# Splits of weights, a tree of squares and one bank: a reordered start of three stages in a hybrid decoder layer

## The chip, the cores and the metric

One core of one Trainium2 chip. The metric is the device time of one execution in microseconds (us); lower is better. TensorE, VectorE (DVE), ScalarE (ACT) and GpSimd (POOL) work side by side, each through its own list of instructions in order, and wait for each other through semaphores. SyncE (SP) issues the loads.

## The reference

One inference step of a decoder layer for 288 tokens (256 of a prompt, 8 sequences of 4), model width 2048, in fp32:

```python
def swiglu(x, w_gate, w_up, w_down):
    return (jax.nn.silu(x @ w_gate) * (x @ w_up)) @ w_down

x = x + 0.5 * rmsnorm(swiglu(rmsnorm(x, g_ffn1_pre), ...), g_ffn1_post)        # FFN 1, inner width 5632
h = rmsnorm(x, g_mix_pre);  p = h @ w_in                                       # q, k, v, o-gate, glu a, b, i-, f-gate
mix = concat[o * mlstm(q, k, v, i, f; C, n, m), silu(layernorm(dwconv31(a * sigmoid(b))))]
x = x + rmsnorm(mix @ w_out, g_mix_post)
x = x + 0.5 * rmsnorm(swiglu(rmsnorm(x, g_ffn2_pre), ...), g_ffn2_post)        # FFN 2
# rmsnorm(x, g) = x * rsqrt(mean(x * x) + 1e-6) * g
```

The mLSTM has 4 heads of 256 with a carried memory C, normaliser n and stabiliser m; its gates run over time as sums and maxima. The outputs are x and the new states.

## The kernel before, in words

Activations lie feature by feature: 16 chunks of 128 features x 288 tokens. All weights come as one stream of 658 pieces of 128 x 1024 numbers (8 blocks of 128 x 128) through four slots (`raw`, `whi`, `wlo`). Each fp32 product is made of three fast ones: ScalarE writes the rounded high half of a piece (`split_hi`, L781), then VectorE or POOL writes the rest (`split_lo`, L1100 on VectorE, L1535 on POOL), which also frees the slot for SyncE's next load (L370). TensorE then multiplies a block with high and low halves of the activations (`multiply`, L408 to L410), three matmuls of 288 columns. `dve_splits` (L131) decides by the piece's number which of VectorE and POOL makes a low half: even numbers go to VectorE, with exceptions at the start of mix and FFN 2 and in the heads. ScalarE takes the high half of piece g only when TensorE is through piece g-4 (`piece_done`).

Three stages begin alike: FFN 1, mix and FFN 2. There the matmuls start before the norm is known: the columns are scaled by `rstd` when a tile is read out of its bank (`evict_scaled`, L1174; `evict` in mix). The first five tiles are multiplied side by side, chunk by chunk (`project_first`, pieces 0 to 9), while VectorE and ScalarE still make the chunks. Then one tile follows another, two pieces each (tile 5 is pieces 10 and 11).

Meanwhile the squares of the 16 chunks lie in `y`. VectorE adds them in a tree of four adds (`square_tree`, L1163: 8, 4, 2 and 1 chunks at a time). TensorE sums the result over the partitions between two chunks of tile 5 (`token_sums`, L450, into bank 4), VectorE and ScalarE make variance, root and reciprocal (L1106, L790, L1109), TensorE spreads the row back over the partitions (`norm_row_to`, L460, bank 4), and ScalarE copies it out (`copy_rstd`, L795). In the FFNs the sums stand after chunk 10 of tile 5 and the row after chunk 15; in mix after chunk 2 of its second piece and after chunk 7 of it (mix counts p = 8, 9 for pieces 10, 11 of the stage).

Tile T goes to bank T % 4; `SPARE_BANK` puts tiles 4, 5, 6 of a stage into banks 5, 6, 7. `tile_start` (L392) makes TensorE wait until the tile four before is evicted; in the loops it asks for T-3 evictions. Tile 7 is in bank 3 and waits for four evictions.

In the FFNs two tiles (gate and up) make one chunk of the hidden layer (`gate_up`): VectorE evicts the gate tile, ScalarE takes the sigmoid (L820), POOL multiplies (L1558), VectorE evicts the up tile, multiplies (L1195), ScalarE copies the high half (L824), VectorE subtracts (L1197). The first four pairs are written out, with the splits that are due in between; the others run in loops, 20 pairs in each of the two halves of both FFNs. ScalarE's functions need the table of their kind: it is loaded (ACT_TABLE_LOAD) before the first Sqrt, Sigmoid, Exp or Ln after another kind. `sqrt_table` puts a dummy Sqrt ahead.

In mix, once `rstd` is there, VectorE scales the gate rows of 4 x 288 (L1289 on), ScalarE takes logs (`gate_logs`) and the sigmoid of the conv input, VectorE scans and subtracts (L1300 to L1316), and ScalarE exponentiates (`gate_rows`), before TensorE spreads these rows (`broadcast_rows`, L533). ScalarE's splits of pieces 15, 16, 17 stand between these in its list. The convolution's taps (L1329) accumulate in bank 4.

Of the kernel before, what the change touches and what calls it, by code (L numbers as in the profile page):

```python
# [52 lines left out]

START_SPLITS = {0: 0, 1: 1, 2: 2, 3: 4, 4: 5, 5: 7, 6: 9, 7: 10, 8: 12, 9: 14}
NEXT_SPLITS = {4: 5, 5: 8, 6: 10, 7: 12, 8: 14, 9: 15}
NEXT_LOW = {4: 7, 5: 9, 6: 11, 7: 13, 8: 15, 9: 16, 10: 16}
LAST_GROUPS = ((0, 4), (4, 8), (8, 10), (10, 12))
LAST_POOL = ((12, 14), (14, 16))
BLOCKS = (0, P, TOK - P)
# [58 lines left out]
def tile_of(h, kind):  # L118
    return HEAD_T + TILE_KINDS.index((h, kind))


SPARE_BANK = {4: 5, 5: 6, 6: 7, GATE_T: 5, tile_of(0, "k0"): 6, tile_of(0, "k1"): 7,
              FFN2_T + 4: 5, FFN2_T + 5: 6, FFN2_T + 6: 7}


def tile_bank(T):
# [4 lines left out]
def dve_splits(g, i=None):  # L131

    if HEAD_P + MIX_FROM + LOOK <= g < HEAD_P + MIX + 8:
        return g - HEAD_P - LOOK in DVE_LO
    if i is None and (GATE_P + 4 <= g <= GATE_P + 12 or FFN2_P + 4 <= g <= FFN2_P + 10):
        return g <= GATE_P + 10 or g >= FFN2_P
    return g % 2 == 0


# [25 lines left out]
def hybrid_layer_kernel(nc, stream, x_in, vecs, gate_vec, c_in, n_in, conv_in,  # L165
                        y_out, cp_out, np_out, cs_out, ns_out, m_out, conv_out):
    with ExitStack() as ctx:
# [223 lines left out]
        def _(pe):  # L391
# [96 lines left out]
            def ffn(g, T, h_from, x_from, sums):  # L488

                for half, n in enumerate(FF_HALVES):  # L490
                    start = 0
                    if half == 0:
                        def square_sum(k):
                            if k == 10:
                                pe.wait_ge(xsq_sum, sums)
                                token_sums(y[:, 0, :], True, True)
                            if k == XC - 1:
                                norm_row_to(2 * sums - 2, (4,))

                        project_first(T, g, x_from)  # L500
                        for q in range(FIRST, CH):
                            project(T + q, g + 2 * q, 0, 0, None, square_sum if q == FIRST else None)
                        start = 2
                    with pe.Fori(start, n // 2) as i:
                        for q in range(4):
                            project(T + q, g + 2 * q, 4, 8, i)
                    T, g = T + 2 * n, g + UP_PIECES[half]
                    tiles = 4 if half == 0 else 8
                    with pe.Fori(0, XC // tiles) as i:
                        down(T, g, 0, tiles, n, tiles, tiles * n // CH, i, h_from)  # L510
                    T, g, h_from = T + XC, g + DOWN_PIECES[half], h_from + n
                return g, T
# [150 lines left out]
            def between(p, j):  # L663


                for h in range(H):
                    k = p - KEYS_AT[h]
                    late = LATE[h] > 0
                    if (k, j) == (6, 2):
                        broadcast_rows(h)  # L670
                    if (k, j) == (9, 2):
                        to_token_major(h)
                    if (k, j) == (13, 1):
                        scores(h)
                    if (k, j) == ((16, 1) if late else (14, 1)):
                        query_memory(h)
                    if (k, j) == (14, 5):
                        denominators(h)
                    if (k, j) == ((17, 5) if late else (15, 5)):
                        attend(h)  # L680
                    b = updates.get((k - LATE[h], j))
                    if b is not None:
                        update_memory(h, b)
                if (p, j) == (MIX_FROM + 1, 2):
                    pe.wait_ge(xsq_sum, 2)
                    token_sums(y[:, 0, :], True, True)
                if (p, j) == (MIX_FROM + 1, CH - 1):
                    norm_row_to(2, (4,))
                if (p, j) == (88, 5):
                    ln_mean()  # L690
                if (p, j) == (92, 2):
                    ln_squares()
# [80 lines left out]
        def _(act):  # L773
# [6 lines left out]
                    act.wait_ge(piece_done, at(g - 3, per, i))  # L780
                act.activation(whi[:, g % SLOTS, :], raw[:, g % SLOTS, :], ACT.Copy).then_inc(hi_ready, 1)  # L781

            def sqrt_table(k):

                act.activation(warm[:, k:k + 1], ones[:, 0:1], ACT.Sqrt)

            def norm_root(k, scale):

# [22 lines left out]
            def ffn(g, T, f_from, sq_from, norm_at):  # L811
                for half, n in enumerate(FF_HALVES):
# [11 lines left out]
                        act.activation(hh[:, k, :], scr[:, 4, :], ACT.Copy).then_inc(h_hi, 1)  # L824

                    if half == 0:
                        sqrt_table(norm_at)
                        for p in range(10, 15):
                            split_hi(g + p)
                        norm_root(norm_at, 1.0)  # L830
                        copy_rstd(norm_at, norm_at + 1)
                        gate_up(None, T, f_from, 0, (g + 15,), (g + 16,))
                        gate_up(None, T + 2, f_from + 1, 1, (), (g + 17,))
                        gate_up(None, T + 4, f_from + 2, 2, (), (g + 18,))
                        gate_up(None, T + 6, f_from + 3, 3, (), ())
# [17 lines left out]
            def down_body(g, T, tiles, n, per, i, half, sq_from, d0, norm_at):  # L853
                t = 0
                for p in range(per):
                    split_hi(g + p + LOOK, per, i)
                    if (p + 1) * CH >= (t + 1) * n:
                        if half == 1:

                            c = d0 + t  # L860
                            if c == XC - 1:
                                sqrt_table(norm_at)
                            act.wait_ge(tile_evicted, T + t + 1)
                            act.wait_ge(ssq_added, SQ_BUFS + sq_from + c - 1)
                            act.activation(sq[:, c % 2, :], y[:, c, :], ACT.Square).then_inc(sq_ready, 1)  # L865
                            if norm_at == 5:
                                act.activation(y[:, c, :], y[:, c, :], ACT.Copy, scale=gain("g_ffn2_post", c))\
                                   .then_inc(y_scaled, 1)
                        t += 1
# [166 lines left out]
            for p in range(MIX_FROM, MIX + 8):  # L1036
                split_hi(HEAD_P + p + LOOK)
                if p == MIX_FROM:
                    sqrt_table(2)
                    norm_root(2, 1.0)  # L1040
                    copy_rstd(2, 3)
                if p == 9:
                    gate_logs()
# [28 lines left out]
            for p in range(8):  # L1072
                split_hi(OUT_P + p + LOOK, 8, XC // 4 - 1)
                if p == 7:
                    sqrt_table(3)
                if p >= 4:
                    out_squares(p - 4, False, XC // 4 - 1)
            norm_root(3, 1.0)
# [12 lines left out]
        def _(dve):  # L1091
# [89 lines left out]
            def ffn(g, T, f_from, norm_at):  # L1181
                for half, n in enumerate(FF_HALVES):
# [15 lines left out]
                           .then_inc(h_ready, 1)  # L1198

                    if half == 0:  # L1200
                        split_lo(g + 12)
                        norm_factor(norm_at)
                        split_lo(g + 14)
                        dve.wait_ge(rstd_ready, norm_at // 2 + 1)
                        gate_up(None, T, f_from, 0, (g + 10, g + 10), (), ())
                        gate_up(None, T + 2, f_from + 1, 1, (g + 10, g + 10), (), (g + 16,))
                        gate_up(None, T + 4, f_from + 2, 2, (g + 10, g + 12), (), (g + 18,))
                        gate_up(None, T + 6, f_from + 3, 3, (g + 14, g + 16), (), ())
                    with dve.Fori(2 - 2 * half, n // 2) as i:
                        for jj in range(2):  # L1210
# [57 lines left out]
            dve.wait_ge(vec_landed, 16)  # L1268
            x_operands(0, "g_ffn1_pre", 0, START_SPLITS)
            split_lo(10)  # L1270
            square_tree(XC)
            ffn(0, 0, 0, 0)
            norm_factor(1)
# [12 lines left out]

            gates, raw_f, raw_i = bank[tile_bank(GATE_T)], bank[4][0:H, 0:TOK], bank[tile_bank(GATE_T)][0:H, 0:TOK]
            log_f, b_run = bank[4][0:H, 0:TOK], bank[tile_bank(GATE_T)][0:H, 0:PADT]
            link(dve.tensor_tensor(raw_f, gates[32:32 + H, 0:TOK], rstd[32:32 + H, :], ALU.mult))  # L1289
            dve.tensor_scalar(g_f, raw_f, gv[:, 1:2], None, ALU.add).then_inc(gf_ready, 1)  # L1290
            dve.tensor_tensor(raw_i, raw_i, rstd[0:H, :], ALU.mult).then_inc(tile_evicted, 1)
# [13 lines left out]
            for k in range(2):  # L1305
                dve.tensor_tensor(compact(rows[:, R_BM:R_BM + TOK], k), padded(b_run, k), padded(mrun, k), ALU.subtract)
                last = dve.tensor_tensor(compact(rowc, k), padded(igp, k), padded(b_run, k), ALU.subtract)
            link(last)
            bm_dec = compact(rows[:, R_BM:R_BM + TOK], 1)
            dve.tensor_tensor(g_arg[:, 0:NS].rearrange("h (b t) -> h b t", b=NB), compact(rowc, 1),  # L1310
                              bm_dec[:, :, NT - 1:NT].broadcast_to([H, NB, NT]), ALU.add)
            dve.tensor_tensor(g_wi[:, 0:NS].rearrange("h (b t) -> h b t", b=NB), bm_dec,
# [39 lines left out]
            def conv_part(h, c):  # L1352

                if c == TAPS_FROM[h]:
                    dve.wait_ge(u_ready, 2 * h + 2)
                    if h:
                        dve.wait_ge(cu_evicted, (NB + 1) * h)
                first = TAP_PAIRS[h] * (c - TAPS_FROM[h])
# [170 lines left out]
        def _(pool):  # L1529
# [21 lines left out]
            def ffn(g, T, f_from, stage, k):  # L1551
                for half, n in enumerate(FF_HALVES):
# [8 lines left out]
                            split_lo(after, 8, i)  # L1561

                    if half == 0:
                        split_lo(g + 11)
                        gate_up(None, f_from, g + 13, g + 15)
                        gate_up(None, f_from + 1, None, g + 17)
                        gate_up(None, f_from + 2, None, None)
                        gate_up(None, f_from + 3, None, None)
                    with pool.Fori(2 - 2 * half, n // 2) as i:
                        for jj in range(2):  # L1570
                            gate_up(i, f_from + jj, g + 4 * jj + 3, g + 4 * jj + 5)
# [56 lines left out]
            pool.affine_select(out=mask4[:, :, :], in_=mask4[:, :, :], compare_op=ALU.is_ge, fill=0.0, base=NT - 1,  # L1628
                               pattern=[[NS, 4], [NT, NB]], channel_multiplier=-1).then_inc(pads_ready, 1)
            pool.memset(ysum[:, :], 0.0)  # L1630
            for p in (11, 12):
                split_lo(GATE_P + p)

            def conv_part(h, c):

# [182 lines left out]
```

## Time and profile before

| | |
|---|---|
| median of 3 runs | 2226.0 us (2225.51 to 2227.9) |
| the profiled execution's own time | 2225.09 us |
| its span, first to last instruction | 2223.4 us |
| granted TensorE clock, mean | 0.993 |
| TensorE / VectorE / ScalarE / POOL busy | 2189.3 / 991.5 / 899.3 / 1042.3 us |
| HBM | 166 GB/s over the span |

"Busy" is time in which an engine has an instruction at work. The clock is a share of full speed: 1.00 is 2.4 GHz and 0.5 is 1.2 GHz, and a stretch in between had both. A wait is put down to the instruction that came last. Rows of the timeline give start and length of an instruction and, in brackets, how long its engine stood idle and for whom. FFN 1 begins at 0, mix at 856, FFN 2 at 1355 us.

### The profile page before, as it was taken

To read this page: it belongs to the slowest core of one execution; us is meant where nothing else is said; L and a number is where in the kernel's file an instruction comes from. 1 tells how busy PE (TensorE), PEld (TensorE's weight loads), DVE (VectorE), ACT (ScalarE), POOL (GpSimd) and SP (SyncE) were. 2 spreads that over 40 slices of the span, in tenths; PEclk is the share of its full clock that TensorE was granted. 3 is DMA by queue.
4 is the path that set the end of the run, shared out by engine and by line. 5 is a ranking of instruction groups with operands and counts; after the bars stand their busy time and mean duration, and the time that the engine had idled before them with its cause. 6 is when DMAs were issued, how large, how long until landed. Compare 5 with 4: busy or idle time off the path is not lost.

```text
span 2223.4 us, 42352 instructions
## 1 busy us (share of the span) xinstructions
PE 2189.3 (98%) x16506; PEld 2175.1 (98%) x16506; DVE 991.5 (45%) x1349; ACT 899.3 (40%) x1158; POOL 1042.3 (47%) x587
## 2 busy tenths in 40 slices
PE   9999999999999999999999999999999999999997
PEld 9999999999999999899999999999999999999997
DVE  6543332223334226877767816634332223343323
ACT  5333433334333335444344545333343333333442
POOL 5444443344444442656656573444444334444443
PEclk9999999999999999999999999999999999999999
DMA  6455455545554554555646354455555555555453
GB/s 226 152 166 166 159 170 170 166 159 167 169 163 160 170 170 134 180 171 201 207 158 221 134 194 133 152 170 163 166 162 171 170 162 160 169 166 164 161 171 108
DMA packets 100457, 371.20 MB, mean 167 GB/s; under 512 B 11136, under 2 KB 13312, under 8 KB 99360
## 3 DMA queue, kind: packets, MB, share of 16 engines
q1 hardware_dynamic: 96336, 349.93, 47.9%
q10 hardware_dynamic: 3920, 20.18, 2.5%
q8 instruction: 52, 0.85, 0.2%
q14 instruction: 21, 0.17, 0.0%
q0 software_dynamic: 128, 0.07, 0.0%
HBM read 357.06 MB, written 13.07 MB: 166 GB/s over the span
## 4 chain that ended last, share of the span: by engine, by line
PE 91%; DVE 5%; ACT 1%; issue 1%; POOL 1%; DMA 1%; SPq 0%; DVEq 0%; ACTq 0%; POOLq 0%
PE bank L408 29%; PE bank L409 29%; PE bank L410 28%; DVE y L1163 1%; DVE wlo L1100 1%; DVE bank L1329 1%; PE bank L711 1%; PE bank L712 1%; PE bank L713 1%; ACT whi L781 1%; DMA raw<-stream 1%; DVE x_res L1139 0%; DVE bank L1136 0%; POOL wlo L1535 0%; DVE xl L1113 0%
## 5 line engine op out<-in xcount | busy, mean ns | idle before, releaser
L1535 POOL TENSOR_TENSOR wlo<-raw,whi 128x1024 fp32r<-128x1024 f32 x363 | 880.2, 2427 | 850.7 <-ACT whi L781 838.7
L408 PE MATMUL bank<-xh,whi 128*128 128x288 f32 x3600 | 1065.3, 296 | 12.0 <-DVE scr L1174 6.6
L409 PE MATMUL bank<-xl,whi 128*128 128x288 f32 x3600 | 1065.4, 296 | 0.0
L410 PE MATMUL bank<-xh,wlo 128*128 128x288 f32 x3600 | 1061.8, 295 | 0.0
L781 ACT ACTIVATE whi<-raw 128x1024 fp32r<-128x1024 f32 x658 | 693.3, 1055 | 637.4 <-PE bank L410 616.0
L1100 DVE TENSOR_TENSOR wlo<-raw,whi 128x1024 fp32r<-128x1024 f32 x295 | 428.4, 1453 | 748.7 <-ACT whi L781 747.7
L408 PEld LDWEIGHTS bank<-xh,whi 128*128 128x128 f32 x3600 | 681.5, 189 | 16.6 <-DVE scr L1174 7.1
L410 PEld LDWEIGHTS bank<-xh,wlo 128*128 128x128 f32 x3600 | 679.5, 189 | 0.0
L409 PEld LDWEIGHTS bank<-xl,whi 128*128 128x128 f32 x3600 | 679.1, 189 | 0.3
L409 PE MATMUL bank<-hl,whi 128*128 128x288 f32 x1408 | 415.4, 295 | 0.0
L410 PE MATMUL bank<-hh,wlo 128*128 128x288 f32 x1408 | 415.0, 295 | 0.0
L408 PE MATMUL bank<-hh,whi 128*128 128x288 f32 x1408 | 412.9, 293 | 0.0
L408 PEld LDWEIGHTS bank<-hh,whi 128*128 128x128 f32 x1408 | 264.7, 188 | 0.0
L409 PEld LDWEIGHTS bank<-hl,whi 128*128 128x128 f32 x1408 | 264.7, 188 | 0.0
L410 PEld LDWEIGHTS bank<-hh,wlo 128*128 128x128 f32 x1408 | 264.5, 188 | 0.0
L1558 POOL TENSOR_TENSOR scr<-scr 128x288 f32<-128x288 f32 x88 | 72.6, 824 | 219.6 <-ACT scr L820 219.6
L824 ACT ACTIVATE hh<-scr 128x288 f32 (+1 forms) x88 | 39.2, 445 | 282.5 <-DVE scr L1195 282.5
L820 ACT ACTIVATE scr<-scr 128x288 f32<-128x288 f32 x88 | 39.2, 445 | 218.7 <-DVE scr L1174 218.7
L1174 DVE TENSOR_TENSOR scr<-bank,rstd 128x288 f32<-128x288 f32 x176 | 80.3, 456 | 81.4 <-PE bank L410 73.8
L1329 DVE SCALAR_TENSOR_TENSOR bank<-upad,vec,bank 128x256 f32<-128x256 f32 x232 | 92.7, 478 | 0.1
L1548 POOL TENSOR_TENSOR ssq<-ssq,sq 128x288 f32<-128x288 f32 x45 | 36.4, 809 | 74.1 <-ACT sq L865 55.8
L1197 DVE TENSOR_TENSOR hl<-scr,hh 128x288 f32 (+1 forms) x88 | 40.3, 458 | 63.7 <-ACT hh L824 63.7
(218 smaller groups left out, 1153.8 us busy)
## 6 DMA issues: line engine op xcount, KB each, us to landing
raw<-stream SPq DMA_DIRECT2D x658, 512.0 KB, 3.4
C<-c_in ACTq DMA_DIRECT2D x4, 2048.0 KB, 9.0
cs_out<-C ACTq DMA_DIRECT2D x4, 2048.0 KB, 8.9
x_res<-x_in SPq DMA_DIRECT2D x4, 576.0 KB, 9.0
conv_out<-upad ACTq DMA_DIRECT2D x4, 302.0 KB, 8.0
y_out<-x_res SPq DMA_DIRECT2D x2, 576.0 KB, 2.8
y_out<-x_res SPq DMA_DIRECT2D x4, 288.0 KB, 2.9
upad<-conv_in ACTq DMA_DIRECT2D x4, 272.0 KB, 3.7
```

Of the source, the lines that this page charges most:

```text
L408: pe.matmul(out, wh, mov_hi[:, k, :], start=first, stop=False)
L409: pe.matmul(out, wh, mov_lo[:, k, :], start=False, stop=False)
L410: return pe.matmul(out, wl, mov_hi[:, k, :], start=False, stop=last)
L781: act.activation(whi[:, g % SLOTS, :], raw[:, g % SLOTS, :], ACT.Copy).then_inc(hi_ready, 1)
L820: act.activation(scr[:, 2, :], scr[:, f % 2, :], ACT.Sigmoid).then_inc(sig_ready, 1)
L824: act.activation(hh[:, k, :], scr[:, 4, :], ACT.Copy).then_inc(h_hi, 1)
L1100: dve.tensor_tensor(wlo[:, g % SLOTS, :], raw[:, g % SLOTS, :], whi[:, g % SLOTS, :].bitcast(F32), ALU.subtract).then_inc(lo_ready[g % SLO ...
L1174: ins = dve.tensor_tensor(out, src, rstd[:, :], ALU.mult)
L1197: dve.tensor_tensor(hl[:, k, :], scr[:, 4, :], hh[:, k, :].bitcast(F32), ALU.subtract)\
L1329: ins = dve.scalar_tensor_tensor(out=out, in0=up_prompt(j, SEQ, k), scalar=w, in1=acc, op0=ALU.mult, op1=ALU.add)
L1535: pool.tensor_tensor(wlo[:, g % SLOTS, :], raw[:, g % SLOTS, :], whi[:, g % SLOTS, :].bitcast(F32), ALU.subtract).then_inc(lo_ready[g % SL ...
L1558: pool.tensor_tensor(scr[:, 5 + f % 2, :], scr[:, f % 2, :], scr[:, 2, :], ALU.mult)\
```

## The change

It touches the first tiles of the three stages.

- `dve_splits`: of the pieces written out at a stage's start, VectorE makes all low halves from 10 (FFN 1) or 4 (mix, FFN 2) up to 18, except 12 and 13; in mix piece 13 and later keep their own rule. New on VectorE are 11, 15 and 17 in FFN 1 and FFN 2 and 11 in mix; new on POOL is 12 in the FFNs. Piece 11 stands before the tree.
- POOL waits for the tree's end (`xsq_sum`) before it splits 12 and 13, and makes no further split in the four written-out pairs.
- The token sums come after chunk 7 of tile 5, the norm row after chunk 12 (mix: after its chunk 7 of the first piece and chunk 4 of the second).
- Tile 7 goes to bank 4 and waits for the copy of `rstd` alone.
- ScalarE loads the Sigmoid table (FFNs) or the Exp table (mix) between the root and the copy of `rstd`.
- In mix's gates the difference `b_run - mrun` of the 32 sample tokens is computed a second time, into bank 4, and two instructions read it there; the taps wait until they have.

```diff
-NEXT_LOW = {4: 7, 5: 9, 6: 11, 7: 13, 8: 15, 9: 16, 10: 16}
+NEXT_LOW = {4: 7, 5: 9, 6: 11, 7: 13, 8: 15, 9: 16, 10: 16, 11: 16}
-SPARE_BANK = {4: 5, 5: 6, 6: 7, GATE_T: 5, tile_of(0, "k0"): 6, tile_of(0, "k1"): 7,
-              FFN2_T + 4: 5, FFN2_T + 5: 6, FFN2_T + 6: 7}
+SPARE_BANK = {4: 5, 5: 6, 6: 7, 7: 4, GATE_T: 5, tile_of(0, "k0"): 6, tile_of(0, "k1"): 7,
+              FFN2_T + 4: 5, FFN2_T + 5: 6, FFN2_T + 6: 7, FFN2_T + 7: 4}
@@ dve_splits
-    if i is None and (GATE_P + 4 <= g <= GATE_P + 12 or FFN2_P + 4 <= g <= FFN2_P + 10):
-        return g <= GATE_P + 10 or g >= FFN2_P
+    if i is None:
+        for begin, n in ((0, 10), (GATE_P, 4), (FFN2_P, 4)):
+            if n <= g - begin <= 18:
+                return g - begin not in (12, 13)
@@ TensorE, ffn
                         def square_sum(k):
-                            if k == 10:
+                            if k == 7:
                                 pe.wait_ge(xsq_sum, sums)
                                 token_sums(y[:, 0, :], True, True)
-                            if k == XC - 1:
+                            if k == 12:
                                 norm_row_to(2 * sums - 2, (4,))
 ...
                         for q in range(FIRST, CH):
+                            if q == CH - 1:
+                                pe.wait_ge(rstd_ready, sums)
@@ TensorE, mix
-                if (p, j) == (MIX_FROM + 1, 2):
+                if (p, j) == (MIX_FROM, CH - 1):
                     pe.wait_ge(xsq_sum, 2)
                     token_sums(y[:, 0, :], True, True)
-                if (p, j) == (MIX_FROM + 1, CH - 1):
+                if (p, j) == (MIX_FROM + 1, 4):
                     norm_row_to(2, (4,))
@@ ScalarE, ffn
                         norm_root(norm_at, 1.0)
+                        load_table(6, ACT.Sigmoid)
                         copy_rstd(norm_at, norm_at + 1)
@@ ScalarE, mix
                     norm_root(2, 1.0)
+                    load_table(7, ACT.Exp)
                     copy_rstd(2, 3)
@@ VectorE, ffn
                     if half == 0:
-                        split_lo(g + 12)
                         norm_factor(norm_at)
                         split_lo(g + 14)
                         dve.wait_ge(rstd_ready, norm_at // 2 + 1)
-                        gate_up(None, T, f_from, 0, (g + 10, g + 10), (), ())
+                        gate_up(None, T, f_from, 0, (g + 10, g + 10), (), (g + 15,))
                         gate_up(None, T + 2, f_from + 1, 1, (g + 10, g + 10), (), (g + 16,))
-                        gate_up(None, T + 4, f_from + 2, 2, (g + 10, g + 12), (), (g + 18,))
+                        gate_up(None, T + 4, f_from + 2, 2, (g + 10, g + 12), (), (g + 17, g + 18))
@@ VectorE, start
             split_lo(10)
+            split_lo(11)
             square_tree(XC)
@@ VectorE, mix
+            bm_dec = bank[4][0:H, 0:NS].rearrange("h (b t) -> h b t", b=NB)
 ...
-            link(last)
-            bm_dec = compact(rows[:, R_BM:R_BM + TOK], 1)
+            link(dve.tensor_tensor(bm_dec, padded(b_run, 1), padded(mrun, 1), ALU.subtract))
@@ VectorE, conv_part
                     dve.wait_ge(u_ready, 2 * h + 2)
+                    dve.wait_ge(args_ready, 1)
@@ POOL, ffn
                     if half == 0:
-                        split_lo(g + 11)
-                        gate_up(None, f_from, g + 13, g + 15)
-                        gate_up(None, f_from + 1, None, g + 17)
-                        gate_up(None, f_from + 2, None, None)
-                        gate_up(None, f_from + 3, None, None)
+                        pool.wait_ge(xsq_sum, k + 1)
+                        split_lo(g + 12)
+                        split_lo(g + 13)
+                        for f in range(CH // 2):
+                            gate_up(None, f_from + f, None, None)
@@ POOL, mix
-            for p in (11, 12):
-                split_lo(GATE_P + p)
+            pool.wait_ge(xsq_sum, 2)
+            split_lo(GATE_P + 12)
```

## Rows read from the trace of the kernel before

**Rows 1.** The page's first part: busy time, share of the span, instructions.

```profile
PE 2189.3 (98%) x16506; PEld 2175.1 (98%) x16506; DVE 991.5 (45%) x1349; ACT 899.3 (40%) x1158; POOL 1042.3 (47%) x587
```

**Rows 2.** Waits of TensorE over the whole run: total, times, longest.

```profile
PE bank L408 <- DVE scr L1174: 6.6, 2, 3.3
PE bank L450 <- DVE y L1163: 4.9, 2, 3.4
```

**Rows 3.** Windows: length, busy of each engine, clock, DMA; steady, then stops.

```profile
57.16:64.32 7.16, 3.86 (x18) 3.70 (x17) 5.72 (x7) 2.27 (x4) 3.82 (x3) 0.76 0.44 147
100.00:150.00 50.00, 50.00 (x380) 50.00 (x380) 19.16 (x25) 19.80 (x24) 22.35 (x12) 1.00 0.51 168
898.31:908.10 9.79, 6.36 (x32) 6.20 (x30) 3.99 (x7) 0.35 (x2) 2.44 (x1) 0.65 0.30 107
...
1409.39:1416.02 6.63, 3.33 (x15) 3.17 (x14) 5.40 (x6) 2.09 (x4) 3.81 (x3) 0.74 0.48 158
```

**Rows 4.** Timeline of TensorE (start, length, instruction, wait): FFN 1, then mix.

```profile
47.50 0.72 PE L450 MATMUL bank<-ones,y 128*128 128x1 f32 x6
48.09 0.38 PE L408 MATMUL bank<-xh,whi 128*128 128x288 f32 x1
...
57.03 0.29 PE L410 MATMUL bank<-xh,wlo 128*128 128x288 f32 x1
60.62 0.41 PE L408 MATMUL bank<-xh,whi 128*128 128x288 f32 x1 [3.29 <-DVE scr L1174]
...
898.18 0.29 PE L410 MATMUL bank<-xh,wlo 128*128 128x288 f32 x1
901.91 0.37 PE L450 MATMUL bank<-ones,y 128*128 128x1 f32 x1 [3.43 <-DVE y L1163]
...
917.24 0.29 PE L410 MATMUL bank<-xh,wlo 128*128 128x288 f32 x1
918.88 0.40 PE L408 MATMUL bank<-xh,whi 128*128 128x288 f32 x1 [1.35 <-POOL wlo L1535]
```

**Rows 5.** VectorE, the tree: FFN 1; first add in mix, second in FFN 2.

```profile
36.61 2.55 DVE L1163 TENSOR_TENSOR y<-y 128x2304 f32<-128x2304 f32 x1
39.20 3.44 DVE L1163 TENSOR_TENSOR y<-y 128x1152 f32<-128x1152 f32 x1
42.68 0.76 DVE L1163 TENSOR_TENSOR y<-y 128x576 f32<-128x576 f32 x1
43.47 0.46 DVE L1163 TENSOR_TENSOR y<-y 128x288 f32<-128x288 f32 x1
...
890.30 4.77 DVE L1163 TENSOR_TENSOR y<-y 128x2304 f32<-128x2304 f32 x1
...
1394.85 1.36 DVE L1163 TENSOR_TENSOR y<-y 128x1152 f32<-128x1152 f32 x1
```

**Rows 6.** Timeline, mix: VectorE splits ahead of the tree, POOL beside it.

```profile
888.03 2.35 DVE L1100 TENSOR_TENSOR wlo<-raw,whi 128x1024 fp32r<-128x1024 f32 x2
...
892.62 4.71 POOL L1535 TENSOR_TENSOR wlo<-raw,whi 128x1024 fp32r<-128x1024 f32 x1
```

**Rows 7.** Timeline, FFN 1: table, product, multiply, fifth eviction.

```profile
52.31 1.28 ACT L820 ACT_TABLE_LOAD   x1
...
55.04 2.57 DVE L1195 TENSOR_TENSOR scr<-scr 128x288 f32<-128x288 f32 x1 [2.71 <-POOL scr L1558]
...
59.49 1.36 POOL L1558 TENSOR_TENSOR scr<-scr 128x288 f32<-128x288 f32 x1 [2.20 <-ACT scr L820]
...
64.39 0.45 DVE L1174 TENSOR_TENSOR scr<-bank,rstd 128x288 f32<-128x288 f32 x1
```

**Rows 8.** Timeline, mix: copy of rstd, high half of 15, gate instruction.

```profile
907.95 0.41 ACT L795 ACTIVATE rstd<-bank 128x288 f32<-128x288 f32 x1 [4.17 <-PE bank L460]
...
915.34 1.04 ACT L781 ACTIVATE whi<-raw 128x1024 fp32r<-128x1024 f32 x1
...
918.80 2.41 DVE L1312 TENSOR_TENSOR gt<-rows,gv 4x32 f32<-4x32 f32 x1
```

More of the change, by code:

```diff
@@ L781, in split_hi, with load_table @@
                 act.activation(whi[:, g % SLOTS, :], raw[:, g % SLOTS, :], ACT.Copy).then_inc(hi_ready, 1)
-            def sqrt_table(k):
-                act.activation(warm[:, k:k + 1], ones[:, 0:1], ACT.Sqrt)
+            def load_table(k, func):
+                act.activation(warm[:, k:k + 1], ones[:, 0:1], func)
             def norm_root(k, scale):
@@ L826, in ffn @@
                     if half == 0:
-                        sqrt_table(norm_at)
+                        load_table(norm_at, ACT.Sqrt)
                         for p in range(10, 15):
@@ L861, in down_body @@
                             if c == XC - 1:
-                                sqrt_table(norm_at)
+                                load_table(norm_at, ACT.Sqrt)
                             act.wait_ge(tile_evicted, T + t + 1)
@@ L1038, in _ @@
                 if p == MIX_FROM:
-                    sqrt_table(2)
+                    load_table(2, ACT.Sqrt)
                     norm_root(2, 1.0)
+                    load_table(7, ACT.Exp)
                     copy_rstd(2, 3)
@@ L1074, in _ @@
                 if p == 7:
-                    sqrt_table(3)
+                    load_table(3, ACT.Sqrt)
                 if p >= 4:
```

## Prediction

> **What bounds the kernel now.** I read the page's head first: TensorE is busy for 98% of the span, the other three engines for less than half [rows 1]. So time can only be won where TensorE stands still or runs at its lower level. Second, the waits of TensorE [rows 2, 4]: three causes carry 12.8 us (6.6 for an eviction in the FFNs, 4.9 for the tree of squares, 1.3 for one split on POOL). Third, the same stretches by windows and by the starts of matmuls [rows 3, 4]. An undisturbed 50 us holds 380 matmuls, 0.1316 us each, 3.16 us a piece (24 matmuls) and 6.32 us a tile. What a stop costs is the distance of starts less what the matmuls between need:
>
> - FFN 1, before the eighth tile (tile 7): starts stand 3.59 us apart, then 0.24 apart instead of 0.13. From 57.03 to 64.19, 16 matmuls apart (the windows count those cut by their edges too), it is 7.16 − 16 × 0.1316 = 5.05 us; the granted clock is 0.76 in this stretch, so part of it was at 1.2 GHz. FFN 2 does the same at 1409: 6.63 − 14 × 0.1316 = 4.79.
> - Mix, token sums: 898.18 to 901.91, and matmuls at 0.24 up to 906.7 (clock 0.65). From 898.18 to 907.97 are 9.79 us; the same instructions take 3.49 undisturbed (a block of token sums 0.59 from start to start, as in FFN 1 [rows 4], a norm row the same, the rest matmuls), loss 6.30. The split of piece 15 at 917.24: 1.64 us between starts, loss 1.6.
> - FFN 2, token sums: the rest of the 4.9 us of waits and 0.2 around it, 1.7, at full clock.
>
> The sum is 5.05 + 4.79 + 6.30 + 1.6 + 1.7 = 19.4 us.
>
> **The change part by part.**
>
> *POOL waits for the tree.* Alone the tree's four adds take 2.55, 1.36, 0.76 and 0.46 us [rows 5]; with 0.04 between them, 5.25. Next to POOL's splits the first took 4.77 and the second 3.44, and POOL's split 4.71 instead of about 2.4 [rows 5, 6]: they take turns. The Trainium skill says so too (SBUF — State Buffer, "Who interferes with whom"): VectorE with two SBUF inputs and a GpSimd instruction that reads SBUF exclude each other for the whole instruction. By that rule, the trace agrees.
>
> Mix: VectorE now takes piece 11 first, 1.18 us (2.35 for two [rows 6]). Piece 11 needs ScalarE's half, which POOL had at 889.88, so it is ready. Tree 891.5 to 896.8, before 890.3 to 901.85. TensorE asks three chunks earlier: 898.31 − 9 × 0.1316 = 897.13. Slack 0.3 us. FFN 2: splits end 1390.1, third 1391.3, tree ends 1396.5, asked at 1396.85, slack 0.3. FFN 1: ScalarE's half of piece 11 comes only at 38.1 (VectorE would be free at 36.7), split until 39.35, tree until 44.6, asked at 46.3, slack 1.7. So the 6.30 and the 1.7 go. The norm row five chunks behind the sums has 2.4 us; sum to variance takes 0.76, root and reciprocal 0.5 more, but in the FFNs ScalarE's first half of piece 14 (1.05) is between, so about 0.6 to 0.8 is left.
>
> *What is queued behind POOL's wait.* The splits of 12 and 13, then the sigmoid multiplies (in mix the memset of wt and the conv products), and behind the splits SyncE's loads of pieces 16 and 17. At 2.4 us each (880.2 us over 363 splits in the groups of the page): mix, 12 until 899.2 and 13 until 901.6; TensorE wants 12 at 901.3 and 13 at 904.5, slack 2.1. FFN 1: 47.0 and 49.4 against 50.7 and 53.9. FFN 2: 1398.9 and 1401.3 against 1401.1 and 1404.3. The loads land about 3.4 us later, at 1404.7 at the latest in FFN 2, where ScalarE can't use piece 17 before TensorE is through piece 13 (1407). Cost nothing; a tree later than these slacks costs TensorE one for one.
>
> *Tile 7 to bank 4.* It no longer waits for four evictions, only for the copy of rstd out of bank 4, now at about 50.2 against a start at 57.16. That removes 5.05 and 4.79. What is late next: tile 8, which wants five evictions at 63.5; before, the fifth came at 64.84 [rows 7], 1.3 us late, so VectorE's chain must be shorter too. I follow it from rstd (norm row 1.2 us earlier: 50.2). ScalarE's half of piece 15 waits for tile 5's end, 50.8, done 51.8; sigmoid at once (its table, 1.28 us [rows 7], was loaded while TensorE ran up to the norm row), 52.3; VectorE splits 15 until 53.0, then POOL's multiply until 53.8, VectorE's product 0.46, h's high half behind ScalarE's half of piece 16 (55.05) at 55.5, low half 56.0. Second pair: eviction, sigmoid 56.95, split 16 until 57.6, multiply 58.4, product, ScalarE's 17 until 58.2, high 59.4, low 59.85, fifth eviction 60.25. Slack 3.2 us. The product that took 2.57 behind POOL's split [rows 7] is 0.46 now, since POOL has no split left until piece 19. Tile 9 wants the sixth at 69.8 and gets it at 63.5, behind splits 17 and 18. Evictions read PSUM and were never held up (0.45 beside a running POOL).
>
> The added splits have a cost that rows bound only from two sides: 1.18 alone, 2.57 behind a POOL instruction. I take 1.18, because POOL has only 0.81 us multiplies there. The other side is also visible: POOL's multiply took 1.36 beside a VectorE split [rows 7], so each may be held for up to 1.2; I took 0.6 to 0.8.
>
> *Tables.* In the FFNs Sigmoid is loaded behind the root, done by 49.8, the norm row is there at 49.7: hidden. In mix Exp is loaded 898.6 to 900.1, before rstd at 900.5; cover gone, 1.3 us at most in a chain with more slack than that.
>
> *Mix gates.* From rstd to ScalarE's half of piece 15 were 7.4 us (907.95 to 915.34 [rows 8]). Now rstd comes at 900.5, so 907.9, less 1.3 for the Exp table: 906.6; POOL's split ends 909.0 to 910.3, wanted at 910.8. The 1.6 us go, with 0.5 to 1.8 to spare. The new subtraction into bank 4 is one 4x32 instruction, 0.17 to 2.41 us (the latter is such an instruction behind POOL [rows 8]); 0.17, because its first operand lies in PSUM. It also frees the two behind it from their 2.00 and 2.41. The arguments come 10 us earlier and TensorE asks for them 8 earlier. The wait for args_ready before the taps is VectorE's on itself, nothing.
>
> **The sum.** 2225.1 (profiled execution; span 2223.4 and 1.7 around it) − 19.4 = 2205.7. The median of the runs is 0.9 above that execution, so 2206.6.
>
> **The rivals.**
>
> *A wait at piece 15 stays.* For: slack 0.5 if the table gains nothing, and ScalarE's queue is rigid there. Against: three table loads became two. 1.6 us: 2208.
>
> *The added splits hold the chain.* Two multiplies held 1.2 each and two splits at 2.57 instead of 1.18 are 2.4 + 2.8 = 5.2 less 1.4 already counted, 3.8 against a slack of 3.2; then TensorE stops 0.6 at tile 8. Only if the products too stay at 2.57 (+4.2) is it 4.8 and then 1.6 at half clock: the gain of tile 7 is gone in both FFNs, 2206.6 + 9.8 = 2216. Against: no POOL split runs there. The Trainium skill (SBUF — State Buffer, same section) speaks for this rival: whoever issues first holds the port to the end, and here VectorE's added split issues ahead of POOL's multiply; the trace has one such pair, at 1.36 [rows 7].
>
> *The trees don't get shorter* (the change doesn't do what it says). Then mix ends its tree at 903.0, a wait of 5.9 and some 2.8 at half clock, FFN 2 at 1400.8, a wait of 3.9 and 1.6: 2206.6 + 8.7 + 5.5 = 2221. Against: FFN 1's first add took 2.55 with POOL idle and mix's 4.77 with POOL at work.
>
> *Slower.* The FFN loops behind the unrolled start: with TensorE 5 us earlier, the other engines could stay late by the same amount in every pair of tiles. There are 80 pairs in loops; from 0.24 us a pair on the gain is eaten, and at 0.3 it would be 2206.6 + 24 = 2231. The place is piece 19: ScalarE reaches it after the fourth pair, at 67.7, POOL is done at 71.2, TensorE wants it at 73.0. Against: the loop is entered with tile 7's eviction 2.4 us after tile 8's start, as before, and a pair lasts 12.6 us in which VectorE works 5 [rows 3].
>
> **How the numbers follow.** Forecast 70%, with its own range 2204.5 to 2207.5. Wait at piece 15: 12%. Chain held: 8%. Trees as long: 5%. Loops: 5%, of which 3 slower by more than 0.2% (4.5 us, about what this measurement tells from nothing) and 2 within. Gains beyond the sum are possible by about 1 to 2 us (0.6 at L556, a load that came late beside C's), so the low end is 2203.5. The first two hold 82%; to cover small waits where slack is 0.3 the high end is 2213.
>
> **What would show it.** The three trees at 5.1 to 5.3 us each. TensorE's waits: no row of scr L1174, y L1163 under 0.5, POOL wlo none; granted clock 1.00 in the windows that had 0.65 to 0.76. L1195 with 0.46 throughout, POOL's L1558 up to 1.4 in the first pairs. The 4x32 gate instructions at 0.17. Wrong it would be if the token sums wait for more than 1 us (a slack of 0.3 misjudged, and one for one), or if a new wait at tile 8 or at piece 12 stands there.

## The result, and the profile after

The changed kernel takes 2204.93 us (median of 4 runs, 2203.2 to 2206.25), the kernel before beside it 2225.76 (4 runs, 2221.55 to 2227.9): ratio 0.9908, 95% interval 0.9891 to 0.9925. The predicted time was 2206.6. The profiled execution took 2204.75 us with a span of 2203.0; before it was 2223.4, so 20.4 us went, where the sum had 19.4.

The busy time of every engine and each engine's share of the chain of work that ended last, from the page of the changed kernel (before, the busy line is in [rows 1]; there the chain had 91% in TensorE):

```profile
PE 2182.3 (99%) x16506; PEld 2169.7 (98%) x16506; DVE 976.8 (44%) x1355; ACT 901.1 (41%) x1161; POOL 1027.6 (47%) x582
...
PE 96%; DVE 2%; issue 0%; POOL 0%; ACT 0%; DMA 0%; SPq 0%; DVEq 0%; ACTq 0%; POOLq 0%
```

TensorE's waits in it (us in total, times, longest). Line numbers are 2 to 7 higher than before: L410 is the old L408, L1169 the tree, L1180 the eviction, L1106 and L1542 the splits on VectorE and POOL, L1201 the product.

```profile
PE bank L410 <- DVE xl L1119: 4.0, 3, 2.3
PE bank L656 <- POOL rpost L1658: 2.3, 1, 2.3
PE bank L447 <- POOL ident L1606: 1.6, 1, 1.6
PE bank L646 <- DVE C L1427: 1.5, 1, 1.5
```

The three rows of [rows 2, 4] are gone: no eviction, no tree, no split of POOL ends a wait. What stays was there before and lies elsewhere. The same stretches by windows (length, TensorE busy with its matmuls, granted clock, DMA), and two that the prediction did not speak of:

```profile
core 0: us, PE busy (x), PEclk, DMA share, GB/s
53.00:60.00 7.00, 7.00 (x55) 1.00 0.51 164
891.00:901.00 10.00, 10.00 (x80) 1.00 0.36 128
1390.00:1400.00 10.00, 10.00 (x78) 1.00 0.59 208
910.90:924.79 13.89, 13.89 (x101) 0.88 0.84 314
1196.26:1201.43 5.17, 2.87 (x21) 1.00 0.21 80
```

The first three hold the places that were at 0.76, 0.65 and 0.74 in [rows 3] (tile 7 starts at 57.59 and at 1394.01 now, the token sums at 892.43); they are at 1.00 and without a gap. The fourth, just behind the spreading of the gate rows, had 1.00 before and now has 0.88.

The timeline of the changed kernel in FFN 1, VectorE, ScalarE and POOL together (start, length, instruction, idle time before it):

```profile
39.72 5.23 DVE L1169 TENSOR_TENSOR y<-y 128x2304 f32<-128x2304 f32 x4
...
45.02 4.73 POOL L1542 TENSOR_TENSOR wlo<-raw,whi 128x1024 fp32r<-128x1024 f32 x2 [9.49 <-DVE y L1169]
...
48.17 1.28 ACT L789 ACT_TABLE_LOAD   x1
...
50.17 0.41 ACT L799 ACTIVATE rstd<-bank 128x288 f32<-128x288 f32 x1 [0.50 <-PE bank L462]
...
52.66 1.23 DVE L1106 TENSOR_TENSOR wlo<-raw,whi 128x1024 fp32r<-128x1024 f32 x1 [1.45 <-ACT whi L785]
...
52.97 1.59 POOL L1565 TENSOR_TENSOR scr<-scr 128x288 f32<-128x288 f32 x1 [3.22 <-ACT scr L824]
...
54.66 0.46 DVE L1201 TENSOR_TENSOR scr<-scr 128x288 f32<-128x288 f32 x1 [0.41 <-POOL scr L1565]
...
58.95 0.46 DVE L1201 TENSOR_TENSOR scr<-scr 128x288 f32<-128x288 f32 x1 [0.41 <-POOL scr L1565]
...
60.30 0.45 DVE L1180 TENSOR_TENSOR scr<-bank,rstd 128x288 f32<-128x288 f32 x1
...
69.39 2.40 POOL L1542 TENSOR_TENSOR wlo<-raw,whi 128x1024 fp32r<-128x1024 f32 x1 [2.07 <-ACT whi L785]
```

And in mix; the last row is the second 4x32 gate instruction of [rows 8]:

```profile
883.36 3.49 DVE L1106 TENSOR_TENSOR wlo<-raw,whi 128x1024 fp32r<-128x1024 f32 x3
...
886.77 5.23 DVE L1169 TENSOR_TENSOR y<-y 128x2304 f32<-128x2304 f32 x4
...
892.09 4.72 POOL L1542 TENSOR_TENSOR wlo<-raw,whi 128x1024 fp32r<-128x1024 f32 x2 [31.37 <-DVE y L1169]
...
893.61 1.28 ACT L789 ACT_TABLE_LOAD   x1
...
895.86 0.41 ACT L799 ACTIVATE rstd<-bank 128x288 f32<-128x288 f32 x1 [0.75 <-PE bank L462]
...
901.97 2.94 ACT L785 ACTIVATE whi<-raw 128x1024 fp32r<-128x1024 f32 x3
...
903.10 4.77 POOL L1542 TENSOR_TENSOR wlo<-raw,whi 128x1024 fp32r<-128x1024 f32 x2 [3.33 <-ACT whi L785]
...
903.72 0.17 DVE L1318 TENSOR_TENSOR gt<-bank,gv 4x32 f32<-4x32 f32 x1
```

A tree is 5.23 us in both and 5.24 in FFN 2, where [rows 5] had 4.77 for the first add of mix alone. All 88 products of L1201 last 0.46; before, four of them lasted 2.55 or 2.57. POOL starts its two splits when the tree ends. TensorE asks for the sums at 892.43, 0.4 us after the tree's end at 892.00; in FFN 1 at 46.74 against 44.95.

### The profile page after: what moved, and what is told of

The parts are those of the page before. It is cut to its first block, busy times and chain, and to the rows that moved or that the text cites. A ratio compares the mean times of both kernels' runs of the same rounds, so it can differ in the third digit from the quotient of the medians.

```text
span 2203.0 us, 42360 instructions
## 1 busy us (share of the span) xinstructions
PE 2182.3 (99%) x16506; PEld 2169.7 (98%) x16506; DVE 976.8 (44%) x1355; ACT 901.1 (41%) x1161; POOL 1027.6 (47%) x582
## 4 chain that ended last, share of the span: by engine, by line
PE 96%; DVE 2%; issue 0%; POOL 0%; ACT 0%; DMA 0%; SPq 0%; DVEq 0%; ACTq 0%; POOLq 0%
PE bank L410 30%; PE bank L411 30%; PE bank L412 30%; DVE bank L1335 1%; PE bank L715 1%; PE bank L717 1%; PE bank L716 1%; PE bank L593 0%; PE bank L650 0%; PE bank L579 0%; PE bank L646 0%; PE bank L447 0%; PE bank L452 0%; DVE ml L1457 0%; POOL wlo L1542 0%
## 5 line engine op out<-in xcount | busy, mean ns | idle before, releaser
L1542 POOL TENSOR_TENSOR wlo<-raw,whi 128x1024 fp32r<-128x1024 f32 x358 | 862.5, 2411 | 854.1 <-ACT whi L785 766.3
L410 PE MATMUL bank<-xh,whi 128*128 128x288 f32 x3600 | 1062.6, 295 | 4.0 <-DVE xl L1119 4.0
L1106 DVE TENSOR_TENSOR wlo<-raw,whi 128x1024 fp32r<-128x1024 f32 x300 | 437.9, 1461 | 749.2 <-ACT whi L785 748.0
L410 PEld LDWEIGHTS bank<-xh,whi 128*128 128x128 f32 x3600 | 679.5, 189 | 7.9 <-issue 5.2
L410 PE MATMUL bank<-hh,whi 128*128 128x288 f32 x1408 | 412.9, 293 | 0.0
L410 PEld LDWEIGHTS bank<-hh,whi 128*128 128x128 f32 x1408 | 264.7, 188 | 0.0
L1180 DVE TENSOR_TENSOR scr<-bank,rstd 128x288 f32<-128x288 f32 x176 | 80.4, 457 | 78.9 <-PE bank L412 74.0
```

The costliest lines, as they stand in the source:

```text
L410: pe.matmul(out, wh, mov_hi[:, k, :], start=first, stop=False)
L1106: dve.tensor_tensor(wlo[:, g % SLOTS, :], raw[:, g % SLOTS, :], whi[:, g % SLOTS, :].bitcast(F32), ALU.subtract).then_inc(lo_ready[g % SLO ...
L1180: ins = dve.tensor_tensor(out, src, rstd[:, :], ALU.mult)
L1542: pool.tensor_tensor(wlo[:, g % SLOTS, :], raw[:, g % SLOTS, :], whi[:, g % SLOTS, :].bitcast(F32), ALU.subtract).then_inc(lo_ready[g % SL ...
```

## The experiments

Ratios are to the kernel before, measured beside each group of runs (medians 2225.29, 2225.9 and 2225.21 us). One execution to the next of the changed kernel itself: three groups gave 2204.93, 2203.1 and 2205.0, so differences under about 2 us are told only where the trace shows their place.

**1. POOL does not wait for the tree.** Theory: this wait carries most of the gain. Rival: the moved splits and the earlier sums do.

```diff
-                        pool.wait_ge(xsq_sum, k + 1)
...
-            pool.wait_ge(xsq_sum, 2)
```

> The changed kernel, but POOL splits 12 and 13 as soon as ScalarE's halves are there, beside the tree. My theory (the port is held in turns): mix's tree goes first add, split 12, second add, split 13, third and fourth add and ends 9.8 us after its start instead of 5.2; TensorE waits about 4.2 us for it in mix and in FFN 2 and 2.9 in FFN 1, and runs some 1.6 to 2.8 us worth at the lower level after each long wait: 2217 to 2223, likeliest 2221. Rival (the earlier piece 11 on VectorE and the bank did it, the order of POOL against the tree matters little): 2205 to 2207.

Measured: 2221.59 us, 0.9982 (0.9972 to 0.9991). TensorE's waits of this kernel, and the start of the sums in mix with the matmul before it:

```profile
PE bank L452 <- DVE y L1169: 9.4, 3, 3.6
```

```profile
896.09 0.29 PE L412 MATMUL bank<-xh,wlo 128*128 128x288 f32 x1
899.95 0.59 PE L452 MATMUL bank<-ones,y 128*128 128x1 f32 x2 [3.56 <-DVE y L1169]
```

The tree lasts 9.34 us in mix instead of 5.23, and all three stages wait for it, 9.4 us in all. Behind each of these waits, and once behind the gate rows, comes a stretch in which the matmuls start 0.24 apart instead of 0.13; the four cost about 6.5 us (the one behind the gate rows has its like in the changed kernel, so 4.3 of it is new). By the ratios (0.9982 against 0.9908) 16.5 us of some 20.5 go with the two added lines, by which POOL waits three times; with both intervals it is 12 to 21. By starts of the same matmuls the two traces differ by 4.1 us in FFN 1, 6.9 around mix's sums and 6.6 at the start of FFN 2. The theory stands, and with it the 2221 of the prediction's third rival as the price of a tree that doesn't shorten.

**2. The wait alone, added to the kernel before.**

```diff
+                        pool.wait_ge(xsq_sum, k + 1)
                         split_lo(g + 11)
...
+            pool.wait_ge(xsq_sum, 2)
             for p in (11, 12):
```

> The kernel before with POOL's wait for the tree, nothing else, so piece 11 is split by POOL after the tree. My theory: mix's tree ends at 895.6 and piece 11 is ready at 898.0, wanted at 897.1: 0.9 us of wait instead of the 6.3 lost at the sums, the wait at piece 15 stays near 1.4; FFN 2 0.9 instead of 1.7; FFN 1 nothing; tile 7's waits stay. 6 to 6.5 gained, 2219.5. Rival (a held split costs what the tree gains, because the wait only changes places): no gain or slower, 2226 or more.

Measured: 2220.83, 0.9979 (0.997 to 0.9988). Its waits, and piece 11 in mix:

```profile
PE bank L408 <- DVE scr L1174: 6.6, 2, 3.3
PE bank L408 <- POOL wlo L1535: 3.8, 3, 1.7
```

```profile
896.35 0.29 PE L410 MATMUL bank<-xh,wlo 128*128 128x288 f32 x1
897.43 0.40 PE L408 MATMUL bank<-xh,whi 128*128 128x288 f32 x1 [0.78 <-POOL wlo L1535]
```

The tree's row is gone, but piece 11, which POOL still splits and now splits late, stops TensorE 0.78 us in mix and 1.7 in FFN 2 (I had expected 0.9 there), and piece 15 stays. So the wait alone is worth 4.7 us by the ratio, and this trace shows piece 11 as what takes part of its gain back. That it pays in full with piece 11 on VectorE ahead of the tree is read from the traces: no run moved piece 11 by itself.

**3 and 4. The eighth tile.** First the changed kernel with tile 7 back in bank 3, then the kernel before with bank 4 alone (the first diff's lines the other way round).

```diff
-SPARE_BANK = {4: 5, 5: 6, 6: 7, 7: 4, GATE_T: 5, ...
-              FFN2_T + 4: 5, FFN2_T + 5: 6, FFN2_T + 6: 7, FFN2_T + 7: 4}
+SPARE_BANK = {4: 5, 5: 6, 6: 7, GATE_T: 5, ...
+              FFN2_T + 4: 5, FFN2_T + 5: 6, FFN2_T + 6: 7}
...
-                            if q == CH - 1:
-                                pe.wait_ge(rstd_ready, sums)
```

> The changed kernel with tile 7 back in bank 3, so it waits for four evictions. My theory: the shorter eviction chain gives the fourth eviction at 58.6 us, tile 7 could start at 57.3: 1.3 us of wait in each FFN and no fall of the clock, 2207.5; up to 3.2 more if the clock falls. Rival (the bank alone removed the 5 us per FFN, the chain nothing): a wait of 3.3 and half clock as before, 2215.

Measured: 2206.93, 0.9912 (0.9899 to 0.9926).

```profile
57.47 0.29 PE L412 MATMUL bank<-xh,wlo 128*128 128x288 f32 x1
58.62 0.40 PE L410 MATMUL bank<-xh,whi 128*128 128x288 f32 x1 [0.85 <-DVE scr L1178]
```

> The kernel before with tile 7 in bank 4 and its wait for rstd, nothing else. My theory: the wait moves to tile 8, which wants the fifth eviction at 63.5 and gets it at 64.9: 1.4 us instead of 5.05 in each FFN, 7.3 gained, 2218.5 (2221.5 if the clock falls in both). Rival (the bank is the whole gain of the FFNs): 9.8 gained, 2216. Rival (the chain is what counts): under 2 gained.

Measured: 2221.59, 0.9985 (0.9976 to 0.9994). TensorE at tile 8 and at piece 19:

```profile
63.81 0.29 PE L410 MATMUL bank<-xh,wlo 128*128 128x288 f32 x1
65.47 0.39 PE L408 MATMUL bank<-xh,whi 128*128 128x288 f32 x1 [1.36 <-DVE scr L1176]
...
74.95 0.29 PE L410 MATMUL bank<-xh,wlo 128*128 128x288 f32 x1
76.14 0.40 PE L408 MATMUL bank<-xh,whi 128*128 128x288 f32 x1 [0.90 <-POOL wlo L1537]
```

In the changed kernel the fourth eviction is late by 0.85 us only, twice. The starts there are 1.15 us apart instead of 0.13, so bank 4 is worth 2 us by the trace; the ratio (0.9912 against 0.9902 to 0.991) can't tell that from nothing. The rest of the 9.8 us at tile 7 comes from the shorter chain of evictions. Bank 4 alone turns two waits of 3.3 into two of 1.36 at tile 8, as the prediction had it (1.3), and two of 0.9 at piece 19, which I had not put into this expectation. Behind all of these waits, in both kernels, the clock stays at 1.00. The gain of bank 4 alone was 3.3 us by the ratio and 4.5 at the two places by starts of matmuls, where I had expected 7.3; removing the stops in full would give 9.8.

**5. Both together on the kernel before**, without moved splits, sums or tables.

> The kernel before with both parts, bank 4 for tile 7 and POOL's wait, but the old division of the splits, old places of the sums and no tables ahead. Theory: mix as in wait_only (5.6 gained), FFN 2's sums 0.8, and per FFN the bank's 5.05 less 1.5 at tile 8 and 1.1 at piece 19: 11.4 gained, 2214; the moved splits are the remaining 9 to 10. Rival (the two parts do it all): 2206 to 2208.

Measured: 2215.43, 0.9957 (0.9944 to 0.9971). Waits: tile 8 1.34 and 1.32, piece 19 0.89 twice, piece 11 0.76 and 1.68, piece 15 1.38. So half of the gain, some 10.5 us, needs the rest of the change. The waits that are left add up to 8.3 us: 5.6 stand behind splits of POOL, 2.7 at tile 8 at the end of the chain of evictions, where VectorE's products still stand behind POOL's splits. That points at who takes which split; it is an argument from these rows and from the small effects in experiments 7 to 9, since no run moved the splits alone.

**6. POOL keeps pieces 15 and 17 in the FFNs.**

```diff
-                return g - begin not in (12, 13)
+                return g - begin not in ((12, 13) if begin == GATE_P else (12, 13, 15, 17))
...
-                            gate_up(None, f_from + f, None, None)
+                            gate_up(None, f_from + f, None, g + 15 + 2 * f if f < 2 else None)
```

> The changed kernel, but POOL keeps pieces 15 and 17 in the written-out pairs of the FFNs, as before the change. My theory: VectorE's products again stand behind POOL's splits (2.6 us instead of 0.46, twice), the fifth eviction comes at 64.3 instead of 60.7, wanted at 63.7: some 0.5 us of wait at tile 8 in each FFN, 2206. Rival (chain has far more slack than I read): no wait, no difference. Rival (the splits on VectorE are what frees tile 8): waits of 1.5 and more, 2208 and more.

Measured: 2207.26, 0.9915 (0.9901 to 0.9929). A product of VectorE behind POOL's split, and TensorE at piece 19:

```profile
54.36 2.40 POOL L1542 TENSOR_TENSOR wlo<-raw,whi 128x1024 fp32r<-128x1024 f32 x1
...
54.51 2.57 DVE L1201 TENSOR_TENSOR scr<-scr 128x288 f32<-128x288 f32 x1 [2.16 <-POOL scr L1565]
...
60.44 2.56 DVE L1201 TENSOR_TENSOR scr<-scr 128x288 f32<-128x288 f32 x1 [0.40 <-POOL scr L1565]
...
63.89 0.45 DVE L1180 TENSOR_TENSOR scr<-bank,rstd 128x288 f32<-128x288 f32 x1
```

```profile
73.97 0.29 PE L412 MATMUL bank<-xh,wlo 128*128 128x288 f32 x1
75.15 0.40 PE L410 MATMUL bank<-xh,whi 128*128 128x288 f32 x1 [0.89 <-POOL wlo L1542]
```

The product is 2.57 again, as in [rows 7], against 0.46 with the splits on VectorE. The chain ends at 64.34, and TensorE starts tile 8 at 64.56 without a wait, so not there, as I expected, but at piece 19 the delay comes out: a wait of 0.9 us in each FFN, 1.15 by starts of matmuls. These 2.3 us are what the trace gives to the two splits; against the changed kernel beside it (2203.1) the median is 4.2 us longer. In the two profiles the rest is a start 0.5 us later and 1.5 us of matmuls at 0.24 behind the gate rows, neither at a place of the moved splits.

**7. No tables ahead.** The two `load_table` calls of Sigmoid and Exp are left out.

> The changed kernel without the two table loads ahead. My theory: in the FFNs nothing (the high half of piece 16 holds ScalarE longer than the table), in mix 1.3 us later at piece 15, whose slack is 0.9: 0.4 us at most, 2205.4. Rival (each table is on the path): three times 1.3, 2209.

Measured: 2205.65, 0.991 (0.9895 to 0.9924). One new wait, at piece 15 of mix:

```profile
PE bank L410 <- POOL wlo L1540: 0.2, 1, 0.2
```

So the Exp table ahead, loaded at 893.61 while TensorE runs on, is what the slack of 0.9 us at piece 15 comes from; in the time 0.2 us can't be seen. The trace has each table load at 1.28 us, with ScalarE's next instruction 0.02 us or less behind it. The Trainium skill (ScalarE: Activation LUTs, "What ACT_TABLE_LOAD costs") puts about as much again on top for a drain; no row of this case shows that.

**8. The gate difference read from SBUF**, without the new subtraction into bank 4.

```diff
-            link(dve.tensor_tensor(bm_dec, padded(b_run, 1), padded(mrun, 1), ALU.subtract))
+            link(last)
+            bm_dec = compact(rows[:, R_BM:R_BM + TOK], 1)
```

> The changed kernel with the gate difference read from SBUF as before, so two 4x32 instructions stand behind POOL's splits of 15 and 16. My theory: the arguments come 4 us later (907.9), the rows at 909.1, wanted at 910.7: no wait, 2205. Rival (the taps and the two evictions behind them on VectorE come late and hold mix's tiles): 1 to 3 us, 2206 to 2208.

Measured: 2202.92, 0.9899 (0.9883 to 0.9915). VectorE there:

```profile
903.49 2.03 DVE L1316 TENSOR_TENSOR gt<-ssq,rows 4x32 f32<-4x32 f32 x1
905.45 2.43 DVE L1318 TENSOR_TENSOR gt<-rows,gv 4x32 f32<-4x32 f32 x1
```

The two 4x32 instructions are 2.03 and 2.43 instead of 0.17 each: with a PSUM operand they pass POOL's split, with both operands in SBUF they wait for it. But nothing waits for them: ScalarE has the rows ready at 909.1 instead of 907.4, and TensorE asks at 910.9. The part is worth nothing here.

**9. The token sums at their old places**, chunk 10 and 15 (mix: the second piece's 2 and 7).

> The changed kernel with the token sums and the norm row at their old places, three chunks later. Theory: the trees end before either place, so no wait; rstd comes 1.2 us later, but the first sigmoid waits for piece 15's high half at tile 5's end anyway, and in mix piece 15's split moves from 0.9 us of slack to 0.3 late: between 0 and 0.5 slower, 2204.5. Rival (rstd's time sets the eviction chain one for one): slack at tile 8 is over 2 us, so still nothing there, but piece 19 would come late: 1 us more.

Measured: 2205.04, 0.9909 (0.9894 to 0.9924), no new wait. The earlier sums gain nothing on top of the rest: they only add slack, and in mix alone. There piece 15 is ready at 908.74 and TensorE takes it at 908.79, so of 0.9 us of slack nearly nothing is left. In FFN 1 the fifth eviction ends at 62.80 instead of 60.75, but this whole execution runs 2.05 us later from its first matmuls on, and TensorE starts tile 8 at 65.99 instead of 63.93: the slack is 3.2 us in both. The tables ahead and the earlier sums thus cover the same place, and leaving out either one costs next to nothing. In experiment 5, without both and without the moved splits, piece 15 stops TensorE for 1.38 us.

**10. The mean of the layer norm later**, aimed at the wait of 2.3 us that stays at L656.

```diff
-                if (p, j) == (88, 5):
+                if (p, j) == (89, 4):
                     ln_mean()
```

> The changed kernel with the LayerNorm mean (L656) asked for seven chunks later, after chunk 4 of p = 89 instead of chunk 5 of p = 88. TensorE now stands 2.3 us there for POOL's sum; seven chunks are 2.8 us of matmuls, and VectorE gets the mean within 0.3 us of the present time. Theory: the whole wait goes, 2.3 us (2.6 with its surroundings) faster than the changed kernel, 2202, and up to 1.6 more on runs where the clock fell behind this wait. Rival (the chain behind the mean is on the path): the wait reappears at the squares (L661) or at conv_ready and nothing is gained.

Measured: 2207.93, 0.9925 (0.9911 to 0.9938), where I had expected 2202; the changed kernel beside it took 2205.0, so this is slower if anything. TensorE's waits, then VectorE and POOL at the place:

```profile
PE bank L661 <- DVE lnb L1473: 3.7, 1, 3.7
```

```profile
1204.29 2.16 DVE L1472 TENSOR_TENSOR lnb<-lnb 128x864 f32<-128x864 f32 x1 [1.56 <-ACT scr L1024]
...
1206.38 5.75 DVE L1473 TENSOR_TENSOR lnb<-lnb,scr 128x288 f32<-128x288 f32 x1
...
1206.91 0.26 POOL L1682 TENSOR_SCALAR_AFFINE_SELECT wt<-wt 32x32 f32<-32x32 f32 x1
...
1207.15 4.66 POOL L1542 TENSOR_TENSOR wlo<-raw,whi 128x1024 fp32r<-128x1024 f32 x2
```

```profile
core 0: us, PE busy (x), PEclk, DMA share, GB/s
1208.14:1212.18 4.04, 0.30 (x3) 0.97 0.43 144
1212.18:1215.58 3.40, 3.40 (x9) 0.53 0.52 172
```

The 2.3 us at L656 went. But the squares' add of 128x288, 0.88 us in the executions of the changed kernel, now falls beside POOL's splits and lasts 5.75, TensorE waits 3.7 for it, and the eight sums behind run at 0.53 and take 3.40 us against 1.72. My expectation saw the removed wait and not which neighbours the moved work would meet, the very thing that the change itself is made of.

**11 and 12. The changed kernel again**, twice.

> The changed kernel once more, as the measure for the others of this call: 2205, between 2203 and 2206.5.

> The changed kernel again, as the measure for late_mean: 2203 to 2206.

Measured: 2203.1, 0.9902 (0.9886 to 0.9917), and 2205.0, 0.991 (0.9895 to 0.9926). Between the first and the last matmuls of the layer, the profile of the first (span 2201.6) has no stretch at half level, that of the second (2203.2) has one, of 8 matmuls, and the one shown above (2203.0) has two.

## Why the prediction was right

Place by place, by starts of the same matmuls in both traces:

| from, to | predicted | measured |
|---|---|---|
| the layer's first matmul to mix | 5.05 | 5.2 |
| mix to the gate rows (L537) | 6.30 + 1.6 | 7.9 |
| gate rows to FFN 2 | 0 | 1.15 |
| FFN 2 | 4.79 + 1.7 | 6.7 |
| ahead of the layer's first matmul | 0 | -0.5 |
| sum | 19.4 | 20.4 |

**The trees**: predicted 5.25, measured 5.23, 5.23 and 5.24. The slacks came out at 0.4 (mix and FFN 2) and 1.8 (FFN 1) where 0.3 and 1.7 were worked out, and the sums never waited. Experiment 1 shows it is POOL's absence that makes them short. One reading was loose: POOL was not idle for the whole of FFN 1's first add (2.55 us from 36.61) in the kernel before. It began a split at 38.20, and that split took 3.23 us instead of 2.4, so there the one that came second paid.

**The chain in the FFNs**: fifth eviction predicted at 60.25, measured 60.75; the 0.5 is the later start of the whole kernel. The multiply behind VectorE's split took 1.59 and 1.37, where I counted 0.8 and named 1.2 us of hold as the bound; the slack of 3 us took it. The second rival (the added splits hold the chain) has its mechanism in the trace and not its price: the multiply is held by 0.6 to 0.8, the product is free at 0.46. The Trainium skill's rule (SBUF — State Buffer, "Who interferes with whom"), that the one that issues first holds the port to its end, fits both rows. Added splits took 1.22 to 1.23 (three in a row in mix 3.49), the lower of my two ends (1.18 and 2.57), as forecast.

**The slower rival**, the loops: piece 19 was ready at 71.8 (predicted 71.2) and no wait stands there. Experiments 4, 5 and 6 show that the place was the right one: each of them waits 0.9 us per FFN exactly there. But once per stage, not in every pair of tiles.

**Mix behind rstd**: ScalarE's three halves start at 901.97, POOL's two splits at 903.10, and piece 15, the first of the two, is ready at about 905.5 where TensorE wants it at 906.4. Slack 0.9, predicted 0.5 to 1.8; the new gate subtraction and the two behind it are 0.17 to 0.18 each, as predicted.

**What was mis-sized** is a term that I set to nothing: the stretch from the gate rows to FFN 2, 1.15 us. None of it is work that the change touches. At 1208.14 before and 1196.26 after, TensorE stops for the same 2.6 us; before, twelve matmuls at 0.24 follow (a window of 6.69 us at a clock of 0.74; the like window above is 5.17 at 1.00), after none. The other way round after the gate rows: 13.89 us at 0.88 against 13.11 at 1.00, with a wait of 0.6 us gone that stood behind a late load. In the two repeats of the changed kernel the same stretch gives 2.65 and 1.16. A second, small slip is in FFN 2's term: between the starts that it uses lie 13 matmuls, not 14, so it is 4.92 and not 4.79, and 4.95 was measured at tile 7. That the sum of a single pair of executions came out within 1 us is in part luck, since spans of the changed kernel alone range from 2201.6 to 2203.2. The remaining 0.7 of the difference to 2206.6 is the step from execution to median: I added 0.9, and the changed kernel's was 0.2.

## What to carry to other kernels

Look for the short chain on the critical path that reads SBUF on VectorE while GpSimd streams its own, and let GpSimd wait for it: taking these waits out of the changed kernel cost 16.5 of some 20.5 us here, though added by themselves they gained 4.7. Before giving a split away or adding such a wait, ask which piece then comes late: bank 4 alone gained 3.3 us, and the delay came out again at the next places, tile 8 and piece 19. A step that is moved meets other neighbours: read what runs beside its new place before its price is taken from the old one.

## What the runs showed that was not expected

- VectorE does not always get its turn. In mix's tree it and POOL alternated, each waiting for the other's current instruction (first add 4.77 us instead of 2.55, split 4.71 instead of 2.4). In the one profile of experiment 10 a 0.88 us add began at 1206.38 and ended at 1212.13, 0.3 us after POOL's second split in a row; POOL ran two selects and two splits back to back meanwhile. The Trainium skill (SBUF — State Buffer, "Who interferes with whom") has the one that issued first hold the port for its whole instruction; by that alone the add would have waited for one instruction of POOL's, 2.4 us at most, and the row says that an engine with work queued can keep the other out for several. Nothing here shows why it happened at this place and not in the trees.
- The lower clock comes or doesn't for the same work. The same gap of 2.6 us was followed by twelve matmuls at 0.24 in the kernel before, eight in one profile of the changed kernel, and none in two. The burst of small matmuls that spreads the gate rows (910.90 to 913.6), with no wait in it, was followed by some thirteen at 0.24 in the profile shown above and by none in the two repeats (clock 1.00 over 908 to 922). Each such stretch costs 0.9 to 1.6 us, and why one comes is open.
